# Recurrence gates of a hybrid encoder layer on 64-row tiles of TensorE, in pairs, with both gates of a block in one matmul

## What is computed

```
xc = centred depthwise conv of the recurrence input        # (tokens, 512)
r  = sigmoid(blockdiag(xc, w_r) + b_r)                     # 8 blocks of 64 x 64
i  = sigmoid(blockdiag(xc, w_i) + b_i)
log_a = -8 * r * softplus(-lambda)
a, b  = exp(log_a), sqrt(1 - exp(2 * log_a)) * i * xc
h = associative scan of h = a * h + b                      # forward, or reverse
```

## Time and profile before

| | |
|---|---|
| timed runs | median 1031.64 us, 1031.17 to 1032.59 |
| profiled execution, its own time | 1032.55 us |
| span of its profile, first to last instruction | 1030.6 us |
| busy in the span | PE 987.4 us, DVE 816.0, ACT 747.0, POOL 335.3 |
| mean granted TensorE clock | 0.988 of 2.4 GHz |
| chain that ended last, by engine | PE 83%, DVE 7%, ACT 4%, issue 3% |

### The profile page before, as it was taken

The page is one execution under the profiler, slowest core; times in us unless marked ns, Lnnn a source line. Parts: engine busy times, 40 slices in busy tenths (PEclk is TensorE's granted clock), DMA queues, the critical chain, the costliest instruction groups (busy, mean ns, idle before and its releaser), DMA issues.

```text
span 1030.6 us, 15287 instructions
## 1 busy us (share of the span) xinstructions
PE 987.4 (96%) x5098; PEld 828.9 (80%) x5098; DVE 816.0 (79%) x1085; ACT 747.0 (72%) x1005; POOL 335.3 (33%) x176
## 2 busy tenths in 40 slices
PE   8999999989999999859999999999999999999995
PEld 7998998867877888748888888888888888888874
DVE  6659898988884226678988998898889888988883
ACT  7557788487994554537977787788779877977773
POOL 1000000043891111040524652464256336603321
PEclk9999999999999999979999999999999999999998
DMA  7111101002103633479999999999999999999852
GB/s 263 48 42 39 43 12 42 1 1 78 47 1 134 237 123 108 166 274 411 408 392 392 402 400 392 392 410 392 381 393 401 383 389 387 408 381 363 303 169 35
DMA packets 75282, 248.47 MB, mean 241 GB/s; under 512 B 9388, under 2 KB 16616, under 8 KB 75240
## 3 DMA queue, kind: packets, MB, share of 16 engines
q1 hardware_dynamic: 70472, 231.12, 58.1%
q0 software_dynamic: 4752, 16.78, 6.5%
q10 hardware_dynamic: 16, 0.00, 0.0%
HBM read 231.11 MB, written 16.78 MB: 241 GB/s over the span
## 4 chain that ended last, share of the span: by engine, by line
PE 83%; DVE 7%; ACT 4%; issue 3%; POOL 1%; DMA 1%; ACTq 0%; SPq 0%; POOLq 0%; DVEq 0%
PE bank L1008 25%; PE bank L1010 25%; PE bank L1009 24%; PE bank L1014 5%; DVE e_lo L1713 2%; ACT e_hi L933 2%; PE bank L1207 1%; PE bank L1173 1%; PE bank L1174 1%; DMA w_raw<-in_w_in_dram 1%; POOL prob L633 1%; PE bank L1058 1%; POOL wo_lo L625 0%; DMA xs<-h_rows,idx_all 0%; DVE row_stat L1542 0%
## 5 line engine op out<-in xcount | busy, mean ns | idle before, releaser
L1008 PE MATMUL bank<-e_hi,xsT_hi 128*128 128x512 f32 x512 | 200.9, 392 | 1.2 <-DVE xsT_lo L1718 1.0
L1009 PE MATMUL bank<-e_lo,xsT_hi 128*128 128x512 f32 x512 | 199.3, 389 | 0.0
L1010 PE MATMUL bank<-e_hi,xsT_lo 128*128 128x512 f32 x512 | 199.3, 389 | 0.0
L665 POOL COPY idx_now<-idx_all 128x1 uint32 (+1 forms) x15 | 156.8, 10454 | 22.5 <-DMA y_dram<-ys,idx_now 22.5
L933 ACT ACTIVATE e_hi<-raw_gate 128x1024 fp32r<-128x1024 f32 x128 | 134.8, 1063 | 33.0 <-PE bank L1010 31.5
L1713 DVE TENSOR_TENSOR e_lo<-raw_down,e_hi 128x1024 fp32r<-128x1024 f32 x128 | 146.9, 1222 | 2.4 <-ACT e_hi L933 0.8
L1713 DVE TENSOR_TENSOR e_lo<-raw_up,e_hi 128x1024 fp32r<-128x1024 f32 x128 | 146.8, 1221 | 1.5 <-ACT e_hi L933 1.3
L1713 DVE TENSOR_TENSOR e_lo<-raw_gate,e_hi 128x1024 fp32r<-128x1024 f32 x126 | 145.8, 1220 | 2.5 <-ACT e_hi L933 2.5
L933 ACT ACTIVATE e_hi<-raw_up 128x1024 fp32r<-128x1024 f32 x128 | 126.5, 1057 | 1.6 <-PE bank L1010 0.3
L933 ACT ACTIVATE e_hi<-raw_down 128x1024 fp32r<-128x1024 f32 x128 | 125.1, 1058 | 1.2 <-PE bank L1010 1.1
L1008 PEld LDWEIGHTS bank<-e_hi,xsT_hi 128*128 128x128 f32 x512 | 96.1, 188 | 21.6 <-DVE xsT_lo L1718 1.2
(11 more groups left out here) (256 smaller groups left out, 2197.2 us busy)
## 6 DMA issues: line engine op xcount, KB each, us to landing
raw_gate<-in_exp_w_gate_dram SPq DMA_DIRECT2D x64, 1024.0 KB, 11.9
raw_up<-in_exp_w_up_dram SPq DMA_DIRECT2D x64, 1024.0 KB, 8.9
raw_down<-in_exp_w_down_dram SPq DMA_DIRECT2D x64, 1024.0 KB, 8.6
w_raw<-in_w_in_dram SPq DMA_DIRECT2D x6, 1024.0 KB, 5.3
wo_raw<-in_w_out_dram SPq DMA_DIRECT2D x8, 512.0 KB, 4.3
y_dram<-x SPq DMA_DIRECT2D x8, 512.0 KB, 5.0
h_rows<-h SPq DMA_DIRECT2D x8, 512.0 KB, 2.8
x_nat<-in_x_prompt_dram SPq DMA_DIRECT2D x4, 512.0 KB, 6.2
```

The lines of the kernel that those rows point to most:

```text
L665: pool.tensor_copy(idx_now[:, 2:3], idx_all[:, bass.ds(e, 1)] if not isinstance(e, int) else idx_all[:, e:e + 1]).then_inc(idx_copied, 1)
L1008: pe.matmul(out, l_hi, r_hi, start=first, stop=False)
L1009: pe.matmul(out, l_hi, r_lo, start=False, stop=False)
L1010: return pe.matmul(out, l_lo, r_hi, start=False, stop=last)
```

## The change

The two diagonal blocks of a ct are no longer one zero-filled 128 x 128 matrix for each gate. Block n (rows 64n to 64n + 63) now has a 64 x 128 matrix with r and i side by side, in the order r, i for n = 0 and i, r for n = 1. A gates step is 2 sequences x 3 parts x 2 blocks = 12 matmuls of 64 rows and 512 columns; two neighbours differ in n, so in the half of the rows that they use, and in the bank that they write. r and i of a block come out on different halves of the partitions, so that each sigmoid is split in two of 64 partitions by 1024. `bd_raw`, `bd_hi` and `bd_lo` are half as wide (128 x 256).

```diff
-    bd_raw = at("bd_raw", R2, [P, 4, P], F32)
-    bd_hi = at("bd_hi", R2 + 2 * K, [P, 4, P], F32R)
-    bd_lo = at("bd_lo", R2 + 4 * K, [P, 4, P], F32R)
+    bd_raw = at("bd_raw", R2, [P, 2, P], F32)
+    bd_hi = at("bd_hi", R2 + 2 * K, [P, 2, P], F32R)
+    bd_lo = at("bd_lo", R2 + 4 * K, [P, 2, P], F32R)
+    assert 2 * BD == P
...
                     for n in range(P // BD):
-                        sp.dma_start(bd_raw[n * BD:(n + 1) * BD, 2 * d + m, n * BD:(n + 1) * BD],
+                        col = (m + n) % 2 * BD
+                        sp.dma_start(bd_raw[n * BD:(n + 1) * BD, d, col:col + BD],
                                       w[0, d, ct * (P // BD) + n, :, :]).then_inc(bd_loaded, 16)
...
-                act.activation(rt[d][:, :], bank[:, 4:6, :].rearrange("p a b -> p (a b)"), ACT.Sigmoid,
-                               bias=vecs[:, V_BR + CT * d + ct:V_BR + CT * d + ct + 1]).then_inc(sigm_done, 1)
+                for n in range(P // BD):
+                    rows = slice(n * BD, (n + 1) * BD)
+                    ins = act.activation(rt[d][rows, :], bank[rows, 4 + 2 * n:6 + 2 * n, :].rearrange("p a b -> p (a b)"), ACT.Sigmoid,
+                                         bias=vecs[rows, V_BR + CT * d + ct:V_BR + CT * d + ct + 1])
+                ins.then_inc(sigm_done, 1)
                 if ct:
                     act.wait_ge(scaled, 2 * (ct - 1) + d + 1)
-                act.activation(ib_of(ct, d)[:, :], bank[:, 6:8, :].rearrange("p a b -> p (a b)"), ACT.Sigmoid,
-                               bias=vecs[:, V_BI + CT * d + ct:V_BI + CT * d + ct + 1]).then_inc(sigm_done, 1)
+                for n in range(P // BD):
+                    rows, other = slice(n * BD, (n + 1) * BD), slice((1 - n) * BD, (2 - n) * BD)
+                    ins = act.activation(ib_of(ct, d)[rows, :], bank[other, 4 + 2 * n:6 + 2 * n, :].rearrange("p a b -> p (a b)"), ACT.Sigmoid,
+                                         bias=vecs[rows, V_BI + CT * d + ct:V_BI + CT * d + ct + 1])
+                ins.then_inc(sigm_done, 1)
...
-                for m in range(2):
-                    for s in range(SEQS):
-                        tok = slice(s * S, (s + 1) * S)
-                        ins = product(bank[:, 4 + 2 * m + s, :], bd_hi[:, 2 * d + m, :], bd_lo[:, 2 * d + m, :],
-                                      xc_hi[:, tok], xc_lo[ct][:, tok], True, True)
+                for s in range(SEQS):
+                    tok = slice(s * S, (s + 1) * S)
+                    for i, (w, x) in enumerate(((bd_hi, xc_hi), (bd_lo, xc_hi), (bd_hi, xc_lo[ct]))):
+                        for n in range(P // BD):
+                            rows = slice(n * BD, (n + 1) * BD)
+                            ins = pe.matmul(bank[:, 4 + 2 * n + s, :], w[rows, d, :], x[rows, tok], start=i == 0, stop=i == 2)
                 ins.then_inc(gates_done, 1)
```

## The result

The changed kernel takes **1037.56 us** (median of 5 runs, 1036.10 to 1040.53) beside 1031.64 us (5 runs, 1030.55 to 1034.77) for the kernel before on the same chip: the ratio is 1.0056, 95% interval 1.0033 to 1.0080. It is slower by 5.9 us where 3.0 was forecast, inside the forecast's range. The profiled execution took 1037.56 us, its span is 1035.8 us.

A forecast was written before the change was run, and what follows sets the result against it. PE was taken to bound the projection stage; after the change the ACT/DVE chain, -6.6 + 5G + 7(B - 4.06), gives +1.35 us, a clock fall +1.6, sum +3.0: 1034.6 us from the median, range 1031.2 to 1040.2.

The forecast's parts named there:

- DVE's slack before the last GELU product: End of the projection stage: DVE waited 1.32 us for the last GELU, so the delay arrives less 1.32.
- The pairs: Gates steps on PE: the two 64-row matmuls of a pair run side by side, six pairs costing 1.40 us.
- G = 1.60: G is PE's time for one gates step, 2.80 us before; forecast 1.6, with bounds 1.40 to 3.5.
- Rival 2: Gates steps: pairs don't overlap, G = 2.80, +7.4 us, 1039.0; +2.8 more if the clock falls; chance 0.20.
- the upper bound: Hand-over between 128-row and 64-row matmuls, in and out of a gates step: at most 2 x 0.36 us.
- So the 9.6 us turn into waits: PE, eight gates steps: the 8 x 1.2 us freed become waits before gates (1,1), (2,1) and (3,1).
- B = 4.06: B is ACT's time for a block's sigmoids, 2.02 us before; four half-height ones 1.02 apart were forecast at 4.06.
- Rival 4: ACT's sigmoids: activations don't overlap, B = 4.48, +2.9 us on either first case, up to +6; no separate chance.
- the first two cases: Pairs with the clock falling (the forecast, 1034.6 us, chance 0.40) and pairs with the clock holding (1033.0 us, chance 0.27).
- The clock: After PE's 4.5 us wait before gates (1,1) the clock halves; that step takes 3.2 instead of 1.6: +1.6 us.
- Rival 3: ACT's sigmoids: half-height activations take half the time, B = 2.03, -7.2 us, 1024.4; chance 0.08.
- PE's own lateness: PE's job 20 in the projection stage starts at 157.0 instead of 156.4, +0.6 us, less than DVE's delay.

The follow-up runs named there:

- e5: Kernel before with each sigmoid split in two of 64 partitions, ordered r and i of partitions 0 to 63, then of 64 to 127: 1042.58 us, timed once.
- e7: Changed kernel with its sigmoids ordered r of block 0, i of block 0, r of block 1, i of block 1: 1040.08 us.
- e10: Changed kernel with 36, 22 and 26 unread identity transposes on PE during its waits before gates (1,1), (2,1) and (3,1): 1036.26 us.
- e1: Changed kernel with two full-height sigmoids instead of four of 64 partitions, the gates left unsorted, so timing only: 1026.08 us.
- e11: Changed kernel with all six matmuls of block 0 issued first, then all six of block 1: 1043.00 us.
- e12: Changed kernel with its 12 matmuls issued in groups of three per sequence and block: 1037.57 us, timed once.
- e2: Kernel before with its two sigmoids split into four of 64 partitions, matmuls as before: 1044.68 us.
- e15: The kernel of e8 with sigmoids computed from tanh as in e13: 1034.77 us.
- e8: Changed kernel in e7's order, where for direction 1 PE and ACT start on each block separately, its matmuls unpaired: 1036.67 us.
- e3: Changed kernel with 36, 8 and 26 unread identity transposes on PE during its waits before gates (1,1), (2,1) and (3,1): 1038.06 us.
- e13: Changed kernel with sigmoids computed from tanh, saving a table load ahead of each decay and adding a bias to its exp: 1036.16 us.

## Why the prediction was right, and where its size was off

The terms of the chain, counted from gates (0,0), forecast and measured (each measured number is a difference of the spans above and in the earlier trace rows):

| stretch | forecast | measured |
|---|---|---|
| to the end of the sigmoids of (0,1) | -0.36 | +0.20 |
| from there to (1,0) | 0 | 0.00 |
| sigmoids (1,0) to (1,1), with the clock | +2.62 + 1.6 | +4.75 |
| to (2,0), half-width bd_hi | -0.25 | -0.24 |
| sigmoids (2,0) to (2,1) | +0.17 | +1.07 |
| to (3,0), half-width bd_hi | -0.15 | -0.24 |
| sigmoids (3,0) to (3,1) | +0.64 | +2.75 |
| DVE's slack before the last GELU product | -1.32 | -1.68 |
| sum, at the opening of attention | +2.95 | +6.61 |

- **The pairs** were right: G = 1.60, the value taken. The Trainium skill (TensorE: Matmul & The Clock Gate, Part 3) says that different row groups run concurrently, and this trace agrees; the step would be 2.80 without. Rival 2 fell. The gain of PE is smaller than forecast, 8 x 1.0 us and not 8 x 1.2, since half of the hand-over lies outside the step: 1.60 - 1.40 = 0.2 us in it and 5.94 - 5.74 = 0.2 in the jobs around it. Together that is 0.4, where the upper bound had 0.7. The Trainium skill (TensorEngine Tiling (Array Packing), Key Properties) says that a change of tiling mode drains TensorE; that page gives no time, and the trace shows these 0.4 us. In the chain the outer part stands once, in job 7: +0.20.
- **"So the 9.6 us turn into waits"** was right but for the size of the gain: waits of 4.64, 1.43 and 3.23 us stand where 4.5, 2.4 and 3 were forecast. A further 1.71 us stands before (1,0), as the forecast's own dates had it (PE would come at 84.7, `xc_lo` at 86.10).
- **B = 4.06 was the step that failed.** It measured 4.51. The prediction took the distance of 1.02 from two sigmoids over the same 128 partitions and carried it to neighbours on different ones. Rival 4's mechanism, B = 4.48, was right. The prediction gave this rival no chance of its own, only a place in the first two cases. The chain holds B seven times: 7 x 0.45 = 3.15 us, most of the 3.66 missing. e5 shows the cause (1.01 on the same partitions, 1.12 otherwise), e7 that a change of the output's half is enough and one of the input's half very likely too.
- **The clock** fell after the first wait, as forecast. The step took 2.86 and not 3.2: at half the clock the pairs are 0.43 apart and not twice 0.233, and the hand-over, 2.86 - 6 x 0.43 = 0.3, does not double either. That is 0.34 less. But it fell again after 3.23 us before (3,1), a wait that the prediction had named and then not priced: 2.82 - 1.60 = +1.22. e10 shows the sum of both, 2.6 us.
- **Rival 3** fell: 64 partitions take 1.11 us, as 128 do. e1 shows what it would have been like with B = 2.03 and pairs: forecast -7.2, measured -6.2 at the opening and -5.7 in the median.
- **PE's own lateness**, forecast as less than DVE's, was so: DVE no longer waits before the last GELU product, its last long wait is for `qk_sq`.
- **Luck.** With B = 4.48 the forecast would have been +5.9, the median's figure. But at the opening of attention the delay is 6.61: the second fall (+1.22) and job 7 (+0.20) stand against the shorter slow step (-0.34) and a larger slack (-1.68, not -1.32), and between 6.61 and the median's 5.9 stand the start and the rest of the program (-1.4), where nothing was forecast, and the 0.9 us by which the profiled execution of the kernel before lay above its median. The range reached it because rival 4 and rival 2 without the clock were inside.

What stays open: how the clock decides in a given place. It fell and held after waits of the same length (last section), what filled one wait moved the fall to another place, and executions of one kernel differ: the changed kernel's five have a mean clock of 0.984 at 1036.10 to 1037.56 us, but 0.979 and 0.977 at 1038.56 and 1040.53. Also open is a layout in which both gates of one block land in one half and the sigmoids stay at full height: it wasn't tried.

## What to carry to other kernels

An activation over half of the partitions costs as much as over all of them, so a matmul that is halved by packing must not scatter its result over more activations than before: here 8 us of PE bought 16 more activations of 1.13 us in a loop of ACT and PE in series. Price such a chain by how often each term stands in it (B seven times, G five), since a small error of a term counts that often. And when PE becomes the early one, price a slow step behind each of its new waits, not behind the first alone.

## What the runs showed of the hardware that was not expected

- Sigmoids overlapped by 0.1 us only where input and output both stayed on the partitions of the one ahead (1.01 to 1.02 against 1.12 to 1.13 apart, at 1024 elements; e1, e5, e7).
- PE started a matmul on free rows ahead of earlier ones on busy rows: the seventh issued with the third (e11, step 2.17 us); in groups of three per block all twelve pair (e12, 1.60 us).
- Going from 128-row to 64-row matmuls and back cost 0.4 us in all per gates step, half of it inside the step (1.60 against 6 x 0.233) and half in the jobs around it (5.94 against 5.74).
- The length of PE's wait alone did not decide a fall of the clock. It fell after 4.64 and 3.23 us (the changed kernel), 4.66, 3.14 and 2.76 (e7), 2.63 and 1.93 (e2), 2.40 (e15), 2.41 (e8), 1.71 (e11) and 1.95 (e3, where PE had been busy for 2.05 of 4.00 us). It held after 3.23 us (e5), 2.33 and 1.95 (e2) and 1.71 (the changed kernel).
- A bias of one value per partition beside such a scale costs an exp of 1024 elements 0.09 us (e13).
